# Prologue of a hybrid attention step: the modulation halves placed between the turned row blocks, with two more load slots and four h buffers

## What is computed

```python
def ada_norm(x, c, norm_g, w_ada, b_ada):
    mod = jax.nn.silu(c) @ w_ada + b_ada
    shift, scale, gate = jnp.split(mod, 3, axis=-1)
    h = rms_norm(x, norm_g) * (1.0 + scale[:, None, :]) + shift[:, None, :]
    return h, gate
# then, for prompt and samples:
#   h @ w_in, cut into queries, keys, values, gates of an NSA and a DSA mixer
#   NSA: compressed, selected and window attention; DSA: indexer scores, top-k, attention
#   y = x + gate * ((sig_n * (o_n * silu(z_n)) @ w_up_nsa + sig_d * (o_d * silu(z_d)) @ w_up_dsa) @ w_out)
#   rms_norm(y, final_g); the new key and value rows are outputs too
```

## Time and profile before

| what | us |
|---|---|
| three runs, median | 644.04 |
| lowest and highest of them | 641.52, 645.61 |
| the profiled execution | 644.17 |
| its span in the profile | 642.4 |
| TensorE busy in the span | 607.2 |

### The profile page before, as it was taken

One profiled execution on the slowest core, in us unless ns is written; L12 is line 12 of the kernel. 1 busy time (PEld: TensorE's weight loads), 2 busy tenths in 40 slices (PEclk: granted clock), 3 DMA queues, 4 the chain that ended last, 5 costly groups with the idle time before them and its releaser, 6 DMA issues.

```text
span 642.4 us, 12591 instructions
## 1 busy us (share of the span) xinstructions
PE 607.2 (95%) x4726; PEld 485.9 (76%) x4726; DVE 342.2 (53%) x945; ACT 261.2 (41%) x637; POOL 160.2 (25%) x218
## 2 busy tenths in 40 slices
PE   3899999999999999999999999999999999999995
PEld 0468777676676887665655667999999999998884
DVE  1326213878878545777766673544232452317773
ACT  5214243333222336666656663534313232223443
POOL 2103641250250436464544432000000000000130
PEclk9889999999999989999989999999999999999998
DMA  9953442232443264000300313334634242334003
GB/s 316 385 198 111 177 158 86 57 126 65 140 122 98 77 161 139 2 1 18 117 0 3 88 45 98 101 108 106 222 92 106 67 111 87 67 112 151 0 13 129
DMA packets 52428, 68.40 MB, mean 106 GB/s; under 512 B 5089, under 2 KB 34969, under 8 KB 52208
## 3 DMA queue, kind: packets, MB, share of 16 engines
q1 hardware_dynamic: 49744, 56.85, 29.2%
q10 hardware_dynamic: 1808, 6.31, 2.8%
q0 software_dynamic: 816, 4.43, 1.7%
HBM read 62.99 MB, written 6.66 MB: 108 GB/s over the span
## 4 chain that ended last, share of the span: by engine, by line
PE 66%; DVE 2%; ACT 1%; POOL 1%; issue 1%; DVEq 0%; ACTq 0%; POOLq 0%
PE psum L1099 29%; PE psum L1286 6%; PE psum L1356 6%; PE psum L1325 5%; PE psum L885 4%; PE psum L887 3%; PE psum L886 3%; PE psum L1199 1%; PE psum L1006 1%; PE psum L1396 1%; PE psum L1294 1%; ACT prob L1649 1%; PE psum L1328 1%; DVE psum L2007 1%; PE psum L1306 1%
## 5 line engine op out<-in xcount | busy, mean ns | idle before, releaser
L1479 ACT ACTIVATE w_hi<-stage 128x1024 fp32r<-128x1024 f32 (+2 forms) x56 | 56.1, 1002 | 159.4 <-PE psum L1099 94.0
L1808 DVE TENSOR_TENSOR w_lo<-stage,w_hi 128x1024 fp32r<-128x1024 f32 x34 | 41.7, 1225 | 110.4 <-ACT w_hi L1479 107.0
L1099 PE MATMUL psum<-hT_hi,w_hi 128*128 128x272 f32 x368 | 76.3, 288 | 0.0
L1099 PE MATMUL psum<-hT_lo,w_hi 128*128 128x272 f32 x368 | 76.2, 288 | 0.0
L1099 PE MATMUL psum<-hT_hi,w_lo 128*128 128x272 f32 x368 | 75.9, 288 | 0.0
L885 PE MATMUL psum<-w_hi,hT_hi 128*128 128x512 f32 (+3 forms) x192 | 70.9, 369 | 2.5 <-DVE hT_lo L1764 2.0
L806 POOL TENSOR_TENSOR w_lo<-stage,w_hi 128x1024 fp32r<-128x1024 f32 (+2 forms) x22 | 44.2, 2009 | 108.7 <-ACT w_hi L1479 108.7
L887 PE MATMUL psum<-w_lo,hT_hi 128*128 128x512 f32 (+3 forms) x192 | 67.9, 354 | 0.0
L886 PE MATMUL psum<-w_hi,hT_lo 128*128 128x512 f32 (+3 forms) x192 | 67.8, 353 | 0.0
L1649 ACT ACTIVATE prob<-psum,softmax_stats 128x31 f32<-128x31 f32 (+6 forms) x136 | 61.6, 459 | 6.9 <-DVE softmax_stats L2007 6.1
L876 POOL TENSOR_TENSOR y<-y,final_g 128x512 f32<-128x512 f32 (+1 forms) x5 | 7.8, 1582 | 217.3 <-ACT merged L1696 217.3
(11 more groups left out here) (323 smaller groups left out, 1141.8 us busy)
## 6 DMA issues: line engine op xcount, KB each, us to landing
stage<-in_w_in SPq DMA_DIRECT2D x14, 1024.0 KB, 5.2
stage<-in_w_ada SPq DMA_DIRECT2D x8, 1024.0 KB, 8.3
stage<-in_w_in SPq DMA_DIRECT2D x10, 512.0 KB, 5.3
staging<-in_x_prompt ACTq DMA_DIRECT2D x4, 512.0 KB, 5.7
qT_plain<-in_w_ada SPq DMA_DIRECT2D x2, 1024.0 KB, 11.1
qT_rot<-in_w_ada SPq DMA_DIRECT2D x2, 1024.0 KB, 12.1
cached<-in_cache_nsa_kv SPq DMA_DIRECT2D x32, 64.0 KB, 2.3
stage<-in_cache_nsa_kv SPq DMA_DIRECT2D x16, 128.0 KB, 2.1
```

Of the source, the lines that this page charges most:

```text
L1099: last = mm(out[:, h, :], left[w][:, k, P * x:P * x + P], halves(mov[m])[:, h, :], start=(k == 0 and w + m == 0), stop=(k == tiles - 1 and ...
L1479: last = A(dst, src, ACT.Copy)
L1808: last = tt(dst, src, hi.bitcast(F32), ALU.subtract)
```

## The change

TensorE's order in the prologue is rewritten. The bias products become a function of their own, `bias(c, out)`, and are issued apart from the halves, two before the first half and two before `first_job(0)`. `turn_mod` takes one chunk at a time (w, half) and waits only for that chunk's copy. The halves of modulation 0, 2 and 1 stand between row blocks, turns and `first_job` steps. Chunk 1 is loaded to two new slots, `cached` and qT_dsa, and chunk 3 to slots 0 and 1. h has four buffers, two of them in `relu_d`, and DVE makes the fourth h before the second lo. POOL clears `iqz` behind modulation 1, and the cached rows wait for it too. DVE's wait for the cleared tiles ahead of its jobs goes.

```diff
--- before.py
+++ after.py
@@ -206,6 +206,8 @@
 CHUNKS = (0, 2, 1, 3)
 FIRST_SLOTS, N_FIRST = 4, 10
 
+ADA_SLOT = {0: (0, 1), 2: (2, 3), 1: (6, 7), 3: (0, 1)}
+
 
 
 H_ORDER = [0, 1, 2, 3, 4, 5, KT, 6, 7]
@@ -221,7 +223,7 @@
     if LOADS[i][:2] == ("w", 0):
         return FIRST_SLOTS + LOADS[i][2]
     if i < N_FIRST:
-        return 2 * (CHUNKS.index(LOADS[i][1]) % 2) + LOADS[i][2]
+        return ADA_SLOT[LOADS[i][1]][LOADS[i][2]]
     return i % SLOTS
 
 
@@ -414,6 +416,7 @@
         c_raw = relu_d[:, :, :].rearrange("p a n -> p (a n)")
         ring = stage + [qT[q][:, :, :].rearrange("p j n -> p (j n)") for q in (PLAIN, ROT)]
         ring += [V_all[:, :, :, :].rearrange("p b t n -> p (b t n)"), score[:, :, :].rearrange("p t n -> p (t n)")]
+        ring += [cached[:, :], qT[DSAQ][:, :, :].rearrange("p j n -> p (j n)")]
         rTs = rT[:, :, R_SAMPLE:R_SAMPLE + PAST]
         ng8 = aT[0:8, 0:P]
         pe32 = aT[0:32, P:2 * P]
@@ -431,7 +434,7 @@
         in_tab, in_tab2, in_c, in_small, in_w2, in_cached = sem("in_tab"), sem("in_tab2"), sem("in_c"), sem("in_small"), sem("in_w2"), sem("in_cached")
         in_x = [sem(f"in_x{t}") for t in range(NT)]
         in_pages = sem("in_pages")
-        loaded = [sem(f"loaded{i}") for i in range(FIRST_SLOTS + 2)]
+        loaded = [sem(f"loaded{i}") for i in range(FIRST_SLOTS + 4)]
         pe_freed = sem("pe_freed")
         hi_made, lo_made = sem("hi_made"), sem("lo_made")
         piece_used = sem("piece_used")
@@ -598,7 +601,7 @@
             return x[:, k, 0:SEQ] if k < KT else x[:, :, SEQ:TOK]
 
         def h_flat(i, k):
-            return rope_b[:, i % 2, :] if k < KT else hS[:, :, :]
+            return (rope_b, relu_d)[i // 2 % 2][:, i % 2, :] if k < KT else hS[:, :, :]
 
         def by_group(x):
             return x.rearrange("p (g j d) -> p g j d", g=2, j=4)
@@ -682,6 +685,7 @@
 
                 if step == 0:
                     sp.wait_ge(in_pages, 16)
+                    sp.wait_ge(mod_done, CHUNKS.index(1) + 1)
                 else:
                     sp.wait_ge(aux_done, AUX_AT[("ikT", 3) if step == 1 else ("raw", (0, 3))] + 1)
                 for n in range(16):
@@ -790,7 +794,6 @@
             pool.memset(kzi[:, :, :], 0.0)
             for q in qS:
                 pool.memset(q[:, :], 0.0)
-            pool.memset(iqz, 0.0).then_inc(zeroed, 1)
             def stores(name, buf, n, m, prompt, sample):
 
                 pool.dma_start(prompt, stg[:, buf, :].rearrange("p (t n) -> p t n", t=NT)[:, 0:4, n[0]:n[1]])\
@@ -806,8 +809,12 @@
                     last = pool.tensor_tensor(dst, src, hi.bitcast(F32), ALU.subtract)
                 last.then_inc(lo_made, 1)
 
-            for n in range(FIRST[1]):
-                split_lo(n)
+            split_lo(0)
+            split_lo(1)
+            pool.wait_ge(mod_done, CHUNKS.index(1) + 1)
+            pool.memset(iqz, 0.0).then_inc(zeroed, 1)
+            split_lo(2)
+            split_lo(3)
             for job in range(6):
                 if job == 1:
                     pool.dma_start(o["win_s"][0, :, 0:PAST - NEW].rearrange("s w x g d -> s (w x g d)"),
@@ -896,12 +903,15 @@
             pe.transpose(bank[6][:, 0:8], ng8, ident[0:8, 0:8])
             pe.transpose(bank[6][:, 8:40], pe32, ident[0:32, 0:32]).then_inc(c_turned, 1)
 
+            def bias(c, out):
+                mm(out[0:32, :], tb("brow", 6)[:, 32 * c:32 * c + 32], bada[:, :], start=True, stop=False,
+                   skip_group_check=True)
+
             def modulation(c, e, out, alone):
 
 
-                if e == 0:
-                    mm(out[0:32, :], tb("brow", 6)[:, 32 * c:32 * c + 32], bada[:, :], start=True, stop=False,
-                       skip_group_check=True)
+                if e == 0 and alone:
+                    bias(c, out)
                 arrived(pe, ("ada", c, e))
                 w = staged(("ada", c, e))[:, :].rearrange("p (k n) -> p k n", k=4)
                 for k in range(4):
@@ -917,16 +927,17 @@
             pe.wait_ge(cT_made, 1)
             pe.wait_ge(small_made, 1)
 
-            def turn_mod(half):
-
-                pe.wait_ge(mod_copied, 2 * half + 2)
-                if half:
+            def turn_mod(w, half):
+
+
+                pe.wait_ge(mod_copied, 2 * half + w + 1)
+                if half and not w:
                     pe.wait_ge(ab_made, 1)
-                for w in range(2):
-                    for k in range(4 * half, 4 * half + 4):
-                        last = mm(bank[7][:, 16 * (w * KT + k):16 * (w * KT + k) + 9],
-                                  mod[:, D * w + P * k:D * w + P * k + P], tb("gsel"), start=True, stop=True)
-                last.then_inc(ab_done, 1)
+                for k in range(4 * half, 4 * half + 4):
+                    last = mm(bank[7][:, 16 * (w * KT + k):16 * (w * KT + k) + 9],
+                              mod[:, D * w + P * k:D * w + P * k + P], tb("gsel"), start=True, stop=True)
+                if w:
+                    last.then_inc(ab_done, 1)
 
             def first_job(k):
 
@@ -946,33 +957,37 @@
                 if i:
                     last.then_inc(piece_used, 1)
 
+            bias(0, bank[5])
+            bias(2, bank[6])
             modulation(0, 0, bank[5], False).then_inc(pe_freed, 1)
             modulation(0, 1, bank[5], False).then_inc(mod_done, 1)
             for t in range(NT):
                 pe.wait_ge(xn_made, t + 1)
             turn_x(0)
+            turn_x(1)
             modulation(2, 0, bank[6], False).then_inc(pe_freed, 1)
-            turn_x(1)
             turn_x(2)
+            turn_x(3)
+            turn_mod(0, 0)
             modulation(2, 1, bank[6], False).then_inc(mod_done, 1)
             for k in range(KT):
                 last = pe.transpose(bank[7][:, 256 + NS * k:256 + NS * k + NS], xs[0:NS, 4, P * k:P * k + P],
                                     ident[0:NS, 0:NS])
             last.then_inc(xs_turned, 1)
-            turn_mod(0)
-            turn_x(3)
+            turn_mod(1, 0)
             turn_x(4)
+            bias(1, bank[5])
+            bias(3, bank[6])
             first_job(0)
+            modulation(1, 0, bank[5], False).then_inc(pe_freed, 1)
             first_job(1)
-            pe.wait_ge(mod_copied, 1)
-            modulation(1, 0, bank[5], False).then_inc(pe_freed, 1)
             modulation(1, 1, bank[5], False).then_inc(mod_done, 1)
             first_job(2)
             modulation(3, 0, bank[6], False).then_inc(pe_freed, 1)
             modulation(3, 1, bank[6], False).then_inc(mod_done, 1)
-            pe.wait_ge(mod_copied, 3)
+            turn_mod(0, 1)
             turn_x(5)
-            turn_mod(1)
+            turn_mod(1, 1)
             first_job(3)
             turn_x(6)
 
@@ -1783,8 +1798,8 @@
             make_h(1)
             lo_of_h(0)
             make_h(2)
+            make_h(3)
             lo_of_h(1)
-            make_h(3)
             lo_of_h(2)
             lo_of_h(3)
             make_ab(1)
@@ -1954,7 +1969,6 @@
                                        imm_value=TAKEN))
                 mask_rest(scoreS[:, :]).then_inc(*tell(sel_made))
 
-            dve.wait_ge(zeroed, 2)
             for job in range(G0):
                 aux(job)
                 if job == 2:
```

## The result

Median 641.02 us in 15 runs (638.25 to 644.01) against 645.56 in 15 runs of the kernel before (641.52 to 646.90). The ratio is 0.9943, 95% interval 0.9922 to 0.9964: 3.7 us less, between 2.3 and 5.0. Executions more than 1.5% above the fastest of the same kernel, a few in e1, e2, e3, e6, e9 and among those of the kernel before, are left out of every median and ratio in this document. The profiled execution has a span of 639.5 us against 642.4.

A forecast was written before the change was run, and what follows sets the result against it. TensorE was taken as the bound, busy 607.2 of 642.4 us. With the clock rising at 35.0, the parts together gain 4.1 us at the start of first_job(3), giving 639.9 us against the median of 644.04; range 636.0 to 645.0.

The forecast's parts named there:

- (a): Rival: in the prologue the clock rises as late as before, gain 2.6 us, total 641.4; chance 0.20.
- milestone: End of the second turned modulation, where first_job(3) begins: 49.83 us before, forecast 45.7, a gain of 4.1 us.
- Part 1: bias(0) and bias(2) ahead of the first half, covered by the load wait: cost nothing, gain 1.84 us behind it.
- Part 2: Order up to the first product: stall gone, but at the old clock the product starts 0.85 us later, at 33.0.
- Part 3: Modulation 1 between first_job steps, four h buffers: at most a short wait at the old clock, 0.8 us at the fast.
- Part 4: Second turn split: the 1.02 us stall on ACT's copy goes; two later waits of 0.7 and 0.5 us stay.
- Part 5: Load slots for chunks 1 and 3: earlier issue buys no earlier landing, worth 0; w(1,0) goes at 41 to 43.
- The sum: first_job(3) by clock rise: at 35.0 gain 4.1 us (45.7), at 38.2 gain 2.6 (47.2), at 31 gain 5.8.
- The open term: When the clock rises in the prologue around the first products: taken as 35.0 us, between 31 and 38.2.
- (b): Rival: the clock rises at once or doesn't fall at 28 us; gain 5.8 or more, 638.2 to 636; chance 0.20.
- (c): Rival: the clock falls in the light stretch behind modulation 3, 42 to 45 us, costing 4.2 us; 645.6; chance 0.12.
- (d): Rival: the gain is lost again on a later wait, such as w(1,1) or DVE's selection; 643 to 644; chance 0.08.

The follow-up runs named there:

- e1: The kernel after with the old load slots and the indexer tile cleared at the start again; median 640.15 us, ratio to before 0.9930.
- e2: The kernel after with two h buffers instead of four and lo 1 ahead of h 3 again; median 641.32 us, ratio to before 0.9935.
- e3: The kernel after with each bias product back ahead of its own first half; median 644.42 us, ratio to before 0.9999.
- e6: The kernel after with modulation(1,0) ahead of first_job(0) and (1,1) ahead of first_job(1); median 639.57 us, ratio to before 0.9947.
- e9: The kernel after with both turned modulations in one piece again, each behind both of ACT's copies; median 641.90 us, ratio to before 0.9947.
- e4: The kernel before with only bias(0) and bias(2) moved ahead of the first half; median 642.83 us, ratio to before 0.9959.
- e5: The kernel after with ACT's last modulation copy ahead of its two DMA issues; median 639.52 us, ratio to before 0.9928.
- e7: The kernel after with three added products, their result unread, in two early TensorE waits; median 640.57 us, ratio to before 0.9937.
- e11: The kernel after with the changes of e5, e6 and e7 together; median 636.22 us, ratio to before 0.9881.
- e12: The kernel after with the changes of e5 and e6 and the old load slots; median 639.30 us, ratio to before 0.9912.
- e8: The kernel after, unchanged, profiled and timed once more; median 641.26 us, ratio to before 0.9956.

## Why the prediction was right, by its own steps

**The size** was right: 4.1 us forecast, 3.7 measured (4.5 by the medians), 641.0 for 639.9. The interval, 2.3 to 5.0 us, holds rival (a) with its 2.6 as well, so the total alone doesn't prove the forecast. There is luck in how near it came: it rested on a milestone 4.1 us early, and the two profiles had it 5.9 and 2.2 us early. The mechanism was right in outline; the wait for ACT and the clock were not.

**Part 1** was right that the two biases hide in the wait for the first load and that modulation(0,1) still ends at 18.0. Of the cover only 0.16 us was left, as the biases began 0.48 us later than before. It priced them at 1.84 us, and e4, which does this alone, gains 1.2 to 4.1: nothing shows that price to be wrong. What it left out is the clock. In the three profiles without the early biases it rose near 25 (24.6 to 25.3), in the eleven with them at 17.0 to 24.4, in seven of these (e1, e2, e5, e7, e11, e12 and after) below 20. I had said "the clock rises about there, as before". That the biases bring it up sooner is likely from this and not shown. That they do it by closing gaps fits badly: e6 had no listed wait up to 18.2 and rose at 23.5, e2 waited 0.79 us for the second load and rose at 19.1.

**Part 2** said the first product would come at 33.0, with two slow biases and no wait on DVE. In e8 that is what happened: 3.62 us for the biases (3.7 forecast) and 32.43. In the first profile the biases were fast, 1.90, and the product came at 28.61 after a wait of 1.14 us. So for one of the clock's two courses the step is right to 0.6 us. The wait is labelled POOL; but POOL was done at 27.96, and DVE's hT_lo ended at 28.51, 0.1 us ahead of the product: it is the same wait on DVE as before. That wait is also what bias(1) and bias(3) fill: e3, without them there, shows it as 2.15 us. No run moves these two alone.

**Part 3**, order and buffers, was priced at nearly nothing at the slow clock: e2 agrees for the buffers; for the order e3 leaves it open.

**Part 4** said that the wait for ACT's copy goes, with 0.1+0.6 for the copy. 0.40 us stayed, because ACT first issues two DMAs, 0.41 and 0.68 us long; I had read the queue's list in the code and not its rows. e5 shows it. The split itself is worth 1.57 less 0.40 at that place (e9), more than the 1.02 I gave. The two waits of 0.7 and 0.5 us behind the milestone stay where the clock stays up (e1, e5, e11, e12); in after it is low there and TensorE comes too late to wait.

**Part 5**, slots at 0, was right (e1, e12), by these runs: the passage of the Trainium skill that I named beside it speaks of who issues a transfer, not of when, and doesn't carry that. The times forecast there held nearly: w(1,0) went at 40.38, the cached rows ended at 60.3, w(1,1) waited for POOL.

**The sum.** Low to 38.2 gave 47.2; e8, low to 38.1, gives 47.63; the 0.40 us of ACT's wait are about the difference. Low to 35.0 gave 45.7; the first profile, low to 34.7 but with fast biases, gives 43.97. What e8 leads by at the milestone, with both rises as before, adds up: two biases less at the fast clock (1.94) and 0.62 us less of waiting for ACT, less 0.28 at the first product, come to 2.3 for the 2.2 measured. The open term was named rightly, and it is open still: the same program went both ways.

**Rivals.** (a) is e8's course, (b) didn't occur as a clock that never falls; the nearest are e1, e2, e6 and e11, low for some 3.4 to 4 us ahead of the milestone. (c) did occur: behind the light stretch the clock fell again, between 42 and 52 us, in after, e2, e3, e4, e6, e7, e8 and e9. It cost little where I had 4.2 us: it fell in a part where TensorE waits for DVE anyway. From the milestone to the samples' products is 8.18 us in after (43.97 to 52.15) and 8.17 before (49.83 to 58.00), with the two waits of 0.7 and 0.5 us gone. Where the clock stayed up (e1, e5, e11, e12) it is 8.17 to 8.19 too, so the low stretch cost nothing there; with one like it the others took 7.96 to 8.54, and e9, low for 6.8 us, 9.14. Up to the end of job 0 0.5 us were lost. (d), a later wait, has nothing for it: "rest" follows the low clock to 0.8 us. The rule on transposes of the Trainium skill, which I had weighed for (a), can't be told here. The clock rose inside turned blocks in before and in e2, ahead of them in after, and behind them in e8, where the eight of 22.34 are slow to the last (421 to 476 ns each) and the turned modulation at 24.10 is where it rises. None of this says which work brought it up.

Why the clock's course differs between executions of one program isn't settled; only two kernels have two profiles.

## What to carry to other kernels

Work without a dependency belongs in the first wait of the engine that bounds the kernel, for its own time; that it also brings the clock up sooner is likely here and not shown. Price each product at the clock of its new place: moving 2 us of biases ahead of the first product costs 2 us or 3.7. And before a loss behind the change is explained, sum the low clock of both profiles: 10 us of it were worth 4 us here, about as much as the change.

## What was not expected of the hardware

The low stretches in mid-kernel differ from run to run and are the largest part of the spread (0 to 20.6 us, 573.3 to 582.1 us of rest); where they stand goes with the program, as two pairs of profiles show. The clock column shows 1.00 at the start of every profile while the same eight matmuls take 1.94 us and later 1.07: durations tell it there, the column doesn't. DVE's subtraction of 128x512 took 1.06 us beside POOL's subtraction (27.45 in after, 1.05 in e8) and 0.69 alone (the earlier trace rows and e4). The Trainium skill ("SBUF — State Buffer", Who interferes with whom) has a reason for this: a DVE instruction with two SBUF inputs contends with a GpSimd instruction that reads SBUF, and whichever is first holds the shared port pair for the whole instruction. The traces agree: POOL ended at 27.96, and DVE's end is 0.55 us behind it, as it is in e8 and in e3.
